# Two layers of a diffusion backbone: rope scores in three rounded passes, and waits re-laid around three slots

## The reference, cut to what matters

```python
q_r = _rope(_rmsnorm(q[..., NOPE_DIM:], mq_g[NOPE_DIM:]), *rope)      # per head, 64 columns
k_r = _rope(_rmsnorm(mkr, mk_g[NOPE_DIM:])[:, :, None, :], *rope)     # shared by the 8 heads
s = einsum('bqhgd,bkhd->bhgqk', concat[q_n, q_r], concat[k_n, k_r]) * QK_DIM ** -0.5
p = softmax(s);  o = p @ v
h = h + gate * (concat(o_c, o_d) * silu(g) @ w_out)
```

## Time and profile before

| | us |
|---|---|
| median of 3 runs | 1457.83 (1456.12 to 1458.51) |
| the profiled execution | 1455.26 |
| its span | 1453.4 |
| TensorE busy | 1404.1 |
| VectorE busy | 1039.9 |
| ScalarE busy | 566.6 |
| GpSimd busy | 354.5 |

### The profile page before, as it was taken

The page is one execution under the profiler, slowest core; times in us unless marked ns, Lnnn a source line. Parts: engine busy times, 40 slices in busy tenths (PEclk is TensorE's granted clock), DMA queues, the critical chain, the costliest instruction groups (busy, mean ns, idle before and its releaser), DMA issues.

```text
span 1453.4 us, 18246 instructions
## 1 busy us (share of the span) xinstructions
PE 1404.1 (97%) x7208; PEld 1134.6 (78%) x7208; DVE 1039.9 (72%) x1246; ACT 566.6 (39%) x826; POOL 354.5 (24%) x333
## 2 busy tenths in 40 slices
PE   5999999999999999998999899999999999999998
PEld 1336888888888878877888688888988878899887
DVE  3384999999999878887888545555645677677554
ACT  2554222222222344433433312214436666666432
POOL 1000543334433021201120133442100135432000
PEclk9999999999999999999999999999999999999999
DMA  9998555564555554445456866651424342323674
GB/s 348 406 371 330 175 174 200 159 208 157 201 162 166 189 180 148 151 154 192 140 185 231 300 204 221 220 189 63 159 87 151 139 145 91 114 94 110 224 239 145
DMA packets 63221, 273.28 MB, mean 188 GB/s; under 512 B 6736, under 2 KB 13088, under 8 KB 43296
## 3 DMA queue, kind: packets, MB, share of 16 engines
q1 hardware_dynamic: 42960, 194.51, 38.1%
q0 software_dynamic: 20176, 77.61, 16.7%
HBM read 257.40 MB, written 14.69 MB: 187 GB/s over the span
## 4 chain that ended last, share of the span: by engine, by line
PE 81%; DVE 9%; DMA 4%; ACT 2%; issue 2%; SPq 1%; POOL 0%; DVEq 0%; ACTq 0%
PE banks L1068 16%; PE banks L1069 16%; PE banks L1072 16%; DMA ada_ring<-in_ada_first 2%; PE banks L2268 2%; PE banks L2269 2%; PE banks L2274 2%; PE banks L1274 2%; DVE wl L1030 2%; PE banks L2025 2%; PE banks L2022 2%; PE banks L2019 2%; PE banks L2293 2%; PE banks L582 1%; DVE ada_acc L417 1%
## 5 line engine op out<-in xcount | busy, mean ns | idle before, releaser
L1068 PE MATMUL banks<-xh,wh 128*128 128x512 f32 (+1 forms) x1296 | 473.4, 373 | 0.0
L1069 PE MATMUL banks<-xl,wh 128*128 128x512 f32 (+1 forms) x1296 | 468.5, 369 | 0.0
L1030 DVE TENSOR_TENSOR wl<-raw,wh 128x2048 fp32r<-128x2048 f32 (+1 forms) x125 | 284.2, 2274 | 104.3 <-ACT wh L1024 104.3
L1024 ACT ACTIVATE wh<-raw 128x2048 fp32r<-128x2048 f32 (+1 forms) x125 | 236.7, 1894 | 241.0 <-PE banks L1072 126.5
L1068 PEld LDWEIGHTS banks<-xh,wh 128*128 128x128 f32 x1296 | 245.0, 189 | 46.4 <-issue 5.7
L1072 PE MATMUL banks<-xh,wl 128*128 128x512 f32 (+1 forms) x1296 | 279.8, 368 | 0.3 <-DVE wl L1030 0.3
L1069 PEld LDWEIGHTS banks<-xl,wh 128*128 128x128 f32 x1296 | 245.1, 189 | 40.3 <-issue 0.2
L1072 PEld LDWEIGHTS banks<-xh,wl 128*128 128x128 f32 x1296 | 227.1, 189 | 41.0 <-DVE wl L1030 0.5
L440 POOL DMA_DIRECT2D ada_w<-in_ada_rest x128 | 69.8, 545 | 486.4 <-DVE ada_acc L429 317.7
L417 DVE SCALAR_TENSOR_TENSOR ada_acc<-ada_w,cond,ada_acc 128x1024 f32<-128x1024 f32 x120 | 166.9, 1391 | 4.8 <-DMA ada_w<-in_ada_rest 2.8
L429 DVE SCALAR_TENSOR_TENSOR ada_acc<-ada_w,cond,ada_acc 128x1024 f32<-128x1024 f32 x90 | 131.4, 1460 | 0.0
(11 more groups left out here) (387 smaller groups left out, 2125.7 us busy)
## 6 DMA issues: line engine op xcount, KB each, us to landing
ada_w<-in_ada_rest POOLq DMA_DIRECT2D x128, 512.0 KB, 4.1
raw<-in_ev_tiles SPq DMA_DIRECT2D x52, 1024.0 KB, 6.5
ada_ring<-in_ada_first SPq DMA_DIRECT2D x32, 1024.0 KB, 12.9
raw<-in_out_tiles SPq DMA_DIRECT2D x16, 1024.0 KB, 6.2
raw<-in_od_wide SPq DMA_DIRECT2D x16, 1024.0 KB, 4.9
raw<-in_od_gates SPq DMA_DIRECT2D x16, 1024.0 KB, 5.0
raw<-in_out_wide SPq DMA_DIRECT2D x16, 1024.0 KB, 5.8
hT<-in_hT POOLq DMA_DIRECT2D x4, 1024.0 KB, 11.9
```

The source lines that it names most:

```text
L1024: nc.scalar.activation(b.wh[:, t % 2, 0:width], b.raw[:, t % 2, 0:width], ACT.Copy).then_inc(s.hi_done, 1)
L1030: nc.vector.tensor_tensor(b.wl[:, t % 2, 0:width], b.raw[:, t % 2, 0:width], b.wh[:, t % 2, 0:width].bitcast(F32), ALU.subtract).then_inc( ...
L1068: nc.tensor.matmul(out, wh[:, k, :], b.xh[:, seg, k, :], start=(k == 0), stop=False)
L1069: nc.tensor.matmul(out, wh[:, k, :], b.xl[:, seg, k, :], start=False, stop=False)
```

## The change

It has five parts.

1. The rope part. From unit 2 on (`ROPE_UNIT`), the two float32 matmuls become six of fp32r: rounded by rounded, rounded by rest, rest by rounded. ScalarE rounds `qr` and `kr` (`rope_highs`) ahead of unit 2's key; GpSimd subtracts (`rope_lows`) in place, over `qr` and `kr`, so it first waits until unit 1's scores are done (`scored`). The units 0 and 1 stay as they were.
2. `ADA_SLOTS`: the last three fetches (33, 41, 49) are in slots 34, 42 and 50.
3. Each `orow` buffer has a landing semaphore of its own (`o_landed`; for the buffers from 7 on those of the ada ring, renamed `ring_landed`), and `o_high` waits for its own row alone.
4. SyncE issues the weight tile 1 of layer 0's output projection behind all the `o` rows and not behind row 11.
5. In layer 1's slots 20 to 23 ScalarE copies the transposed queries (`keep_queries`) ahead of the next weight tile's rounding and not behind it.

```diff
-O_LAND = (0, 1, 2, 3, 4, 5, 6, 0, 1, 2, 3, 4, 0, 1, 2, 3)
-O_LANDED = (2, 2, 2, 2, 2, 1, 1, 2, 2, 2, 2, 2, 3, 3, 3, 3)
...
+    b.qrh = put("qrh", "U", 52 * K, [P, 2, 4, P], F32R)
+    b.krh = put("krh", "C", 4 * CORE_COLS + 2 * K, [P, T], F32R)
+    b.qrl = put("qrl", "S", 32 * K, [P, 2, 4, P], F32R)
+    b.krl = put("krl", "S", 36 * K, [P, T], F32R)
...
-ADA_SLOTS = (9, 17, 25, 33, 41, 49)
+ADA_SLOTS = (9, 17, 25, 34, 42, 50)
...
+def o_landed(s, n):
+
+    slot = O_SLOT[n]
+    if slot < ORING:
+        return s.out_o_in[slot], 16 * O_SLOT[:n + 1].count(slot)
+    i = slot - ORING
+    return s.ring_landed[i], 16 * (len(range(i, ADA_PIECES, ADA_RING)) + 1)
...
-    act.wait_ge(s.out_o_in[O_LAND[n]], 16 * O_LANDED[n])
+    act.wait_ge(*o_landed(s, n))
...
         for n in range(11, KT):
-            if n == 12:
-                load_raw(sp, b, s, t0 + 1, out_weights(g, 1), (KT, P))
             load_o(sp, b, s, g, n)
+        load_raw(sp, b, s, t0 + 1, out_weights(g, 1), (KT, P))
...
 def kq_splits(j):
-    return L0_SPLITS + (2 * (j + 1) if j < 8 else j + 10)
+    return L0_SPLITS + (2 * (j + 1) if j < 8 else j + 10) + (2 if j >= ROPE_UNIT else 0)
...
+        def rope_lows():
+            first = kq_splits(ROPE_UNIT) - 4
+            pool.wait_ge(s.scored, L0_UNITS + ROPE_UNIT)
+            for n, (low, full, high) in enumerate(((b.qrl, b.qr, b.qrh), (b.krl, b.kr, b.krh))):
+                pool.wait_ge(s.kq_high, first + n + 1)
+                nc.gpsimd.tensor_tensor(low[:], full[:], high[:].bitcast(F32), ALU.subtract).then_inc(s.kq_low, 1)
+
         def key_query_lows(j):
+            if j == ROPE_UNIT:
+                rope_lows()
...
-                for r in range(2):
-                    half = slice(64 * r, 64 * r + 64)
-                    last = nc.tensor.matmul(ps[2 + r], b.qr[half, head, pair, :], b.kr[half, :], start=False, stop=True)
+                passes = ((b.qr, b.kr),) if j < ROPE_UNIT else ((b.qrh, b.krh), (b.qrh, b.krl), (b.qrl, b.krh))
+                for n, (q, k) in enumerate(passes):
+                    for r in range(2):
+                        half = slice(64 * r, 64 * r + 64)
+                        last = nc.tensor.matmul(ps[2 + r], q[half, head, pair, :], k[half, :], start=False,
+                                                stop=(n == len(passes) - 1))
...
+        def rope_highs():
+            act.wait_ge(s.q_kept, 8)
+            act.wait_ge(s.odd_kr, 1)
+            for high, full in ((b.qrh, b.qr), (b.krh, b.kr)):
+                a.activation(high[:], full[:], ACT.Copy).then_inc(s.kq_high, 1)
...
+            if i - 1 in QUERY_TURN:
+                for r in range(2):
+                    keep_queries(QUERY_TURN[i - 1], r, 4 + r, 2 * (i - 20) + r + 1)
             split_high(nc, act, b, s, t0 + i + 1, l1_width(i + 1))
...
-            if i - 1 in QUERY_TURN:
-                for r in range(2):
-                    keep_queries(QUERY_TURN[i - 1], r, 4 + r, 2 * (i - 20) + r + 1)
```

More of the change, by code:

```diff
@@ L527, in _ @@
             sp.dma_start(b.ada_ring[p % ADA_RING], g.ada_first[p].rearrange("p (h k n) -> p h k n", h=2, k=2)).then_inc(
-                s.ada_pe_landed[p % ADA_RING], 16)
+                s.ring_landed[p % ADA_RING], 16)
             if p == 2:
@@ L577, in ada_matmuls @@
             grp, r = divmod(p, 4)
-            pe.wait_ge(s.ada_pe_landed[p % ADA_RING], 16 * (p // ADA_RING + 1))
+            pe.wait_ge(s.ring_landed[p % ADA_RING], 16 * (p // ADA_RING + 1))
             if r == 0 and grp > 0:
@@ L1366, in _ @@
                 n = ADA_SLOTS.index(i)
-                if i == 33:
+                if i == 34:
                     pe.wait_ge(s.rs_step, 2)
-                if i == 41:
+                if i == 42:
                     pe.wait_ge(s.rs_step, 5)
@@ L1825, in load_o @@
         sp.wait_ge(s.out_o_low, max(m for m in range(n) if O_SLOT[m] == O_SLOT[n]) + 1)
-    sp.dma_start(b.orow[O_SLOT[n]][:], g.o_d[k]).then_inc(s.out_o_in[O_LAND[n]], 16)
+    sp.dma_start(b.orow[O_SLOT[n]][:], g.o_d[k]).then_inc(o_landed(s, n)[0], 16)
 def o_high(nc, act, b, s, n):
@@ L2087 @@
 FIRST_UNIT = 23
+ROPE_UNIT = 2
 FIRST_GATE = L1_TILES - KT
@@ L2642, in keep_output @@
             a.activation(b.qo[:, unit_head(j), :], ps[6][:, 0:256], ACT.Copy).then_inc(s.odd_out, 1)
+        def rope_highs():
[3 more added lines that the diff above has]
+                a.activation(high[:], full[:], ACT.Copy).then_inc(s.kq_high, 1)
         def key_query_highs(j):
+            if j == ROPE_UNIT:
+                rope_highs()
             if j < 8:
@@ L2889, in semaphores @@
     s.ada_lat = sem("ada_lat")
-    s.ada_pe_landed = [sem(f"ada_pe_landed{i}") for i in range(ADA_RING)]
+    s.ring_landed = [sem(f"ring_landed{i}") for i in range(ADA_RING)]
     s.ada_pe_used = sem("ada_pe_used")
```

## The result

| | before | changed |
|---|---|---|
| median of 6 runs, us | 1458.83 (1456.12 to 1459.54) | 1447.19 (1443.42 to 1449.54) |
| ratio, with its 95% interval | | 0.9921 [0.9903, 0.9939] |
| the same kernel measured again, 6 runs | 1455.53 (11 runs) | 1446.15, ratio 0.9933 [0.9917, 0.9948] |
| the profiled execution, its span | 1455.26, 1453.4 | 1449.54, 1447.7 |

The account below looks back on a forecast made before the run. TensorE's waits on the ada fold, `o_high` and copied queries, with clock falls behind them, were taken as the bound. Terms -7.1, -4.7 and -0.3 sum to -12.1 us: 1445.7 from 1457.83, stated as 1445.5, range 1441 to 1451.

Parts of the forecast that it names:

- A: Ada slots: TensorE's wait on the fold in slot 41 goes, full clock returns, VectorE just follows; -7.1 us.
- B: Output projection: rows start on their own landings, weight tile 1 goes behind them; -4.7 us, -7.0 if the clock holds.
- the term -7.0: Output projection's tile 1 starts between 821.1 and 822.3 instead of at 828.69; -7.0 us in the middle.
- The charge for the clock: Before the output projection's tile 1, TensorE stands some 3 us and its clock falls again; 2.3 us charged.
- Rival 2: Weight tile 1 shares the queue and takes 8.8 us to land, a new long wait; 1448.7 us, chance 0.12.
- rival 1: The clock does not fall before the output projection's tile 1; 1443.4 us, chance 0.27.
- C: Rope passes and query copies: gains -1.8 us, delay at unit 2 +1.5, copies nothing; -0.3 us in all.
- the gain of a unit: Three fp32r rope passes, array halves working together, save 0.36 us a unit; five units give -1.8 us.
- rival 3: The six rope passes go one after the other, costing +3.1 us with the delay; 1449 us, chance 0.08.
- The +1.5: Unit 2's slot: ScalarE's roundings delay VectorE's chain, overlapping GpSimd's queue before `outputs` 0; +1.5 us once.
- Rival 5: Slower: VectorE stretches GpSimd's rope subtractions and the work queued behind, so `outputs` 0 stands; 1465 us, chance 0.02.

Follow-up runs that it names:

- e11: The changed kernel itself measured once more, unaltered: median 1446.15 us, ratio 0.9933 to the kernel before.
- e9: The changed kernel, with GpSimd issuing the output projection's first two ada pieces only after weight tile 1 landed: 1447.50 us, ratio 0.9937 to before.
- e5: The changed kernel with GpSimd's two rope subtractions cut to 16 columns and the rounded pair multiplied three times: 1448.23 us, one measurement.
- e8: The changed kernel with the three rope passes from unit 3 on, their preparation moved to slot 25: 1447.94 us, ratio 0.9940 to before.
- e6: The changed kernel with the rope loops changed over, three passes of one array half and then three of the other: 1449.39 us, one measurement.
- e7: The changed kernel, with SyncE waiting for weight tile 1 to land before issuing the residual row and tile 2: 1447.21 us, ratio 0.9931 to before.
- e3: The kernel before with only the rope part in three rounded passes from unit 2 on: 1457.21 us, ratio 1.0001 to before.
- e2: The kernel before with only the per-row landing semaphores and weight tile 1 issued behind the rows: 1453.62 us, ratio 0.9972 to before.

## Why the prediction was right, by its own steps

**A: right.** -7.1 forecast, -7.08 to -7.13 in the ten profiles that have it. VectorE followed, with 0.2 us to spare.

**B: right in mechanism, its two sizes off.** The landings, the early drain and the issue at 809.5 came as worked out. The landing of tile 1 was taken at 6.1 us and was 8.2: the term -7.0 measured -5.0 (the start of tile 1 at 819.68, against 828.69 less the 4.0 us that slot 51 was earlier). The charge for the clock was 2.3 us and is 1.6 where it fell. In sum -3.2 in the changed kernel's profile, -4.9 in e11's, against -4.7. That e11 comes so near is luck: the tile was 2 us later than I had it, and the clock that I took to fall did not. Rival 2's long landing was thus half true, and rival 1's clock that stays up was true in four of nine profiles. Unforeseen was the wait on row 11, beside which GpSimd issues 1 MB of ada pieces. Before, these were issued at 807.97 and 808.55 and had landed by 813.57, ahead of row 11 at 814.26; the earlier row met them. They make tile 1 1.1 us later (e9).

**C: this step failed.** -0.3 forecast, +1.1 measured. The term that was mis-sized is the gain of a unit. It was to be 0.36 us, and is 0.155: the transposes of units 3, 4 and, at the last, 7 start 5.17, 5.32 and 5.79 us earlier than before. I set three passes of 0.23 us against a time of 1.06 that holds 0.1 us more at the first pass of the group and 0.1 at the last. The fp32r form has these too: 1230.31 to 1231.20 is 0.34 + 0.23 + 0.32. Concurrency, the point in dispute with rival 3, was right.

The three terms of C can be read from how far the starts of the transposes lie ahead of before's. The lead is 6.91 us at the border, 6.66 at unit 0's transposes (1190.85 for 1197.51), 5.00 at unit 2's (1216.95 for 1221.95) and 5.79 at the last. So the copies cost 0.25 us, inside -1 to +1; the delay was +1.66 where I had +1.5; and five units gave back 0.79 where I had 1.8, unit 2's own gain being swallowed by the wait, as forecast. The +1.5 was near by luck. I had ScalarE's roundings delay VectorE's chain by all of it, and they delay it by 0.6 us; GpSimd's work beside VectorE adds 0.4 at the negated maximum and 1.1 at the divisions, and some 0.4 of the sum fell into an idle stretch of VectorE's. GpSimd's own queue, which I had end beside it, was ready a microsecond before `outputs` 0. The wait of 2.33 us also brought the clock down to 0.50, which I had not charged; it cost nothing there, as unit 2's transposes wait 0.6 us in place of 1.4 (e5).

**GpSimd beside VectorE.** Rival 5 had the right pair of engines and the wrong loser. VectorE's `nb` ended with GpSimd's instruction in the changed kernel (1196.84 and 1196.82), in e5 (1197.43 and 1197.41) and in e8 (1209.96 and 1209.93). The sentence that the prediction took from the Trainium skill, GPSIMD Engine Reference, Specifications, is half of what stands there: beside VectorE's instructions with two SBUF inputs it names those in a 2-port mode. The fuller rule stands in the Trainium skill, SBUF — State Buffer, Who interferes with whom: the shared pair of ports is held for a whole instruction by whoever starts first, and tensor_scalar can be one of VectorE's forms that needs it. By that rule, the trace agrees in the three pairs of ends above; that `nb` and `prob` ran in such a mode is not seen in a trace.

**The total.** -12.1 forecast; the stages of the changed kernel's profile give -8.9, those of e11's -10.5. Set on the median of 1457.83, as the sum was, they give 1447.4 to 1448.9, and the median is 1447.19. The two profiled executions alone would have said 5.7 us, because before's had the better start. The forecast of 1445.5 is 1.7 us from the median, and it is term A, exact, that carries it; B and C together were forecast at -5.0 and measured -2.1 in the changed kernel's profile and -3.8 in e11's.

## What to carry to other kernels

Before a transfer or a subtraction is put into an engine's idle time, look at who runs beside it: here ScalarE's roundings and GpSimd's subtractions delayed one chain by 1.66 us, and the passes that they prepared saved 0.8. When an earlier start is bought by faster landings, price the landing with what is then in flight beside it: the tile took 8.2 us where it had taken 6.1. And compare two profiles stage by stage from a common pass; here their start alone differed by 3 us.

## What the runs showed of the hardware that I had not expected

- The clock behind a wait of TensorE of 2.3 to 2.5 us before tile 1 fell to about 0.5 in two of six profiles (changed, e6) and stayed at 1.00 in four (e5, e7, e8, e11); behind 2.8, 3.0 and 3.5 us it fell in all three. The length of the wait alone does not decide it: behind the wait of 2.3 us at `outputs` 0 it fell in all six profiles that have it (changed, e3, e6, e7, e9, e11), and in e2 it fell in tile 0 behind waits of 0.3 and 0.7 us. Where it fell before tile 1, tile 1's first 32 matmuls took 9.0 us in place of 7.4.
- A small TENSOR_SCALAR of VectorE's on SBUF (128x2, 0.17 us) can last until GpSimd's instruction ends (0.56 us in e5, 0.61 in the changed kernel, 1.25 in e8), while its reductions from PSUM beside the same GpSimd work kept their 1.2 us (1207.47 to 1208.68 in e8).
- Six matmuls on half arrays took 0.9 us in either program order.
